# Four experts instead of three loaded in the route stage of a mixture-of-experts kernel, with its tables moved

## The reference

```python
scores = sigmoid(xt @ router)                       # 384 tokens x 64 experts
idx = top 8 of scores + bias, within the 4 best of 8 groups
w = scores[idx] / sum(scores[idx]) * 2.5
routed = sum over the 8 of w * (silu(x @ wg[e]) * (x @ wu[e])) @ wd[e]
x = layernorm(ALPHA * x + gate * (routed + shared expert))
```

## Time and profile before

| | us |
|---|---|
| median of 3 runs | 2140.08 |
| lowest and highest | 2138.03, 2142.44 |
| profiled execution, its own time | 2145.58 |
| its span from first to last instruction | 2143.9 |

### The profile page before, as it was taken

One profiled execution on the slowest core, in us unless ns is written; L12 is line 12 of the kernel. 1 busy time (PEld: TensorE's weight loads), 2 busy tenths in 40 slices (PEclk: granted clock), 3 DMA queues, 4 the chain that ended last, 5 costly groups with the idle time before them and its releaser, 6 DMA issues. The chain is left out here.

```text
span 2143.9 us, 19511 instructions
## 1 busy us (share of the span) xinstructions
PE 1703.3 (79%) x6984; PEld 872.7 (41%) x6984; DVE 696.3 (32%) x1257; ACT 338.9 (16%) x765; POOL 379.5 (18%) x276
## 2 busy tenths in 40 slices
PE   3649788784899997888884578966999978898855
PEld 0117647644444433333331366634444433333321
DVE  0014244767422211111114736485313111111117
ACT  0003162000111111111111215300111111111110
POOL 0000000125111111222215300071111111111115
PEclk8769896585999998999997688976999989999988
DMA  9973001033799999999985401307799999999946
GB/s 370 432 311 115 32 11 45 0 123 155 294 369 405 413 413 407 408 402 398 405 325 208 151 11 40 112 31 292 303 404 408 400 411 404 403 385 390 388 181 236
DMA packets 113716, 589.23 MB, mean 275 GB/s; under 512 B 23152, under 2 KB 25200, under 8 KB 61520
## 3 DMA queue, kind: packets, MB, share of 16 engines
q1 hardware_dynamic: 83088, 512.39, 59.1%
q0 software_dynamic: 30528, 75.55, 9.4%
HBM read 575.09 MB, written 48.41 MB: 291 GB/s over the span
## 5 line engine op out<-in xcount | busy, mean ns | idle before, releaser
L1984 PE MATMUL bank<-weights,scratch 128*64 128x512 f32 x448 | 222.7, 655 | 82.4 <-DMA scratch<-in_moe_w_up 47.5
L2091 DVE TENSOR_TENSOR scratch<-scratch,bank 128x256 f32<-128x256 f32 x88 | 54.0, 614 | 674.5 <-ACT scratch L2059 648.6
L1985 PE MATMUL bank<-scratch 128*64 128x512 f32 x480 | 234.1, 645 | 0.0
L1984 PEld LDWEIGHTS bank<-weights,scratch 128*64 128x64 f32 x448 | 65.1, 151 | 229.0 <-issue 229.0
L1984 PE MATMUL bank<-scratch 128*64 128x512 f32 x288 | 131.9, 612 | 17.8 <-DMA scratch<-in_moe_w_up 17.8
L2059 ACT ACTIVATE scratch<-bank 128x256 f32<-128x256 f32 x88 | 33.7, 383 | 707.8 <-PE bank L1985 427.0
L1990 PE MATMUL bank<-weights,scratch 128*128 128x512 f32 x320 | 141.9, 596 | 2.8 <-ACT scratch L2054 1.7
L1763 POOL DMA_INDIRECT y_rows<-hP,y_idx x42 | 43.5, 1036 | 483.6 <-DVE hP L2096 433.8
L1985 PE MATMUL bank<-weights,scratch 128*64 128x512 f32 x256 | 121.1, 629 | 0.0
L1990 PE MATMUL bank<-scratch 128*128 128x512 f32 x256 | 112.9, 594 | 0.0
L1758 POOL DMA_INDIRECT hP<-h_rows,tok_idx x82 | 85.2, 1040 | 149.0 <-PE bank L1719 85.2
(11 more groups left out here) (320 smaller groups left out, 2846.0 us busy)
## 6 DMA issues: line engine op xcount, KB each, us to landing
weights<-in_moe_w_gate SPq DMA_DIRECT2D x64, 1024.0 KB, 14.5
weights<-in_moe_w_up SPq DMA_DIRECT2D x64, 1024.0 KB, 16.3
weights<-in_moe_w_down SPq DMA_DIRECT2D x64, 1024.0 KB, 21.1
scratch<-in_moe_w_gate SPq DMA_DIRECT2D x64, 1024.0 KB, 12.6
scratch<-in_moe_w_up SPq DMA_DIRECT2D x64, 1024.0 KB, 21.9
scratch<-in_moe_w_down SPq DMA_DIRECT2D x64, 1024.0 KB, 18.8
wmod_more<-in_w_mod SPq DMA_DIRECT2D x9, 3072.0 KB, 32.0
weights<-in_w_mod SPq DMA_DIRECT2D x7, 3072.0 KB
```

Of the source, the lines that this page charges most:

```text
L1984: nc.tensor.matmul(out[0:HALF, :], x[:, 0:HALF], w0[:, kk], start=(kk == 0), stop=(kk == KT - 1))
L1985: m = nc.tensor.matmul(out[HALF:P, :], x[:, HALF:P], w1[:, kk], start=(kk == 0), stop=(kk == KT - 1))
L2091: nc.vector.tensor_tensor(B.h[b % 2].rearrange("p (j q) -> p q j", j=2), B.ex[b % 2].rearrange("p (q j) -> p q j", j=2), k.ps[2 + b % 2][: ...
```

## The change

`FIXED` goes from 3 to 4, with a semaphore of its own for the fourth. Experts 0 to 3 get ranks 0 to 3, the loop in the route stage issues the loads of all four, and the loop in the expert stage begins with place 4. The planner, unchanged itself, puts four experts first and spreads 14 sole experts in place of 15 between the pairs. Since slot 3 is now loaded while the router works, the route tables are moved out of it, to the columns behind the router bias, from 576 on; they must end at column 2816, where slot 2 begins. Their 2092 columns end at 2668.

```diff
-FIXED = 3
-FIXED_SEM = (1, 2, 0)
+FIXED = 4
+FIXED_SEM = (1, 2, 0, 5)
 SOLO = 18
 PAIRS = (NE - SOLO) // 2
...
-        self.s_ahead = [ctx.enter_context(nc.semaphore(f"ahead{i}_loaded")) for i in range(5)]
-        self.ahead = [0] * 5
+        self.s_ahead = [ctx.enter_context(nc.semaphore(f"ahead{i}_loaded")) for i in range(6)]
+        self.ahead = [0] * 6
...
     L = LateTables(k)
-    o = 8960
+    o = MOE_BIAS + NE
...
     Pm = cut(NE)
-    assert o <= 15104, o
+    assert o <= 2816, o
```

## The result

The changed kernel takes 2149.14 us in the median of 7 runs (2147.29 to 2155.74), the kernel before 2141.34 us in the median of 7 (2138.03 to 2145.18). The ratio is 1.0035, with a 95% interval of 1.0018 to 1.0052: slower by 7.5 us (an interval of 3.9 to 11.1 us), where 6 us more were forecast.

A forecast was written before the change was run, and what follows sets the result against it. TensorE was taken to pace the expert stages' opening, DMA the rest. Per layer 1.3 to 5.0 us later, taken as 3.0, gave +6 us for two layers: median 2140.1 to 2146, range 2132 to 2156 (forecast's own 2142.7 to 2150).

The forecast's parts named there:

- No idle DMA time in the route stage: Route stage, 522 to 556 us: DMA engines busy without a gap at 414 GB/s, nothing for a fourth expert to fill.
- The cost of the tables and of SyncE's issues: Route stage: moved tables cost nothing; three more issues take SyncE some 1.5 us, covered by 18 us, so nothing.
- One load earlier: Route stage: of the fourth expert's loads only its down load is truly earlier, 2.5 us more work before the gap.
- The opening, 1.3 us behind: Expert stage's beginning, to 612 us: 25 loads served against 25.5 before, so 0.5 load or 1.3 us behind.
- The shared block, up to 5.0 us behind: Shared block 9, ending about 670 us: 43 loads asked for against 45, a lag of up to 2 loads, 5.0 us.
- my 3.0: Each layer's expert stage: 3.0 us later, taken as about the middle between 1.3 and 5.0 us.
- The order behind block 16 changes nothing: Expert stage from block 17 on: only which of a single and a pair comes first differs; nothing added to the sum.
- The amplified rival: Expert stages: eight places with two pairs in a row, before seven; one more 3.6 us wait per layer; 2153; chance 0.08.
- The lag goes into TensorE's waits: DMA-paced part, after 780 us: TensorE's waits for loads grow by 1 to 5 us per layer, no operation added.
- a sign against me: Expert stages: the prediction would be wrong if TensorE stalls before 780 us or its waits for loads fall.
- The gain: Expert stages: 1 to 3 loads of 2.5 us per layer leave the DMA-paced part; -5 to -15 us; chance 0.18.
- Absorption: DMA-paced part: a DMA lag of 1 to 5 us disappears in the slot-release loops; 2140 us; chance 0.22.

The follow-up runs named there:

- b_order: The kernel before with only the changed order of blocks (four sole experts first), three experts loaded in the route stage, tables unmoved: ratio 1.0033, +7.1 us.
- j_shared9: The changed kernel with the second and third shared tile one block later, behind a pair: ratio 1.0017, +3.6 us against the kernel before.
- c_swap: The changed kernel with the order of the kernel before restored from block 6 on: ratio 1.0019, +4.1 us against the kernel before.
- h_early: The kernel before, three experts loaded in the route stage, with the change's order in blocks 0 to 16 only: ratio 1.0026, +5.6 us.
- i_late: The kernel before, three experts loaded in the route stage, with the change's order in blocks 17 to 43 only: ratio 1.0015, +3.2 us.
- d_change: The changed kernel measured again, on another occasion beside other runs on the same chip, against the kernel before: ratio 1.0041, +8.8 us.
- a_tables: The kernel before with only the route tables moved as in the change, three experts loaded in the route stage: ratio 0.9999, no difference.
- x_full: The kernel before with two more 1 MiB copies per layer, HBM to HBM, issued behind place 40: ratio 1.0040, +8.6 us.
- e_pairs3: The kernel before, three fixed experts, with pairs drawn forward in the order of blocks: ratio 1.0005, +1.1 us.
- g_shared: The kernel before with the second and third shared tiles moved later, to blocks 13 and 17: ratio 0.9996, no difference.

## Why the prediction was right, point by point

**No idle DMA time in the route stage.** Right: the share while the router works is 1.00 before and 1.01 after.

**The cost of the tables and of SyncE's issues.** Nothing, as said. But the three issues took 4.88 + 2.53 + 2.53 = 9.9 us, not 1.5: with that many loads outstanding SyncE is held at the issue itself. It was still covered: the last ends at 532.95 us, and the next issue comes with the stage's beginning, 542 us in this execution.

**One load earlier.** It was counted as 2.5 us more work before the gap, already taken off the opening's lag. b_order, which lacks it, does not differ from the change by more than the noise. One step of this sum is off: with all fifteen loads served at 558.5 us and 2.5 us for each, the twelve queued ones last to 551 us, not 553.5. Nothing rests on it.

**The opening, 1.3 us behind.** Right in sign and size: 0.7 MB (1.7 us) behind in layer 0. The bytes moved in these five stretches are 13.6 MB where I had said 14.0, before 14.6; part of the difference is the 0.2 MB moved early at the higher rate.

**The shared block, up to 5.0 us behind.** Right: 4.7 us behind at its end, and the dip deepened as foretold. With j_shared9, which gives back only this, and c_swap, which restores the late order too, about half of the loss is gone. The whole stage is longer by 4.6, 4.3 and 4.6 us in layer 0 (three profiles with this order) and by 1.7, 4.2 and 3.3 us in layer 1, in the mean 3.8. But this term covers only what is made before block 17, and h_early measures that: 5.6 us, 2.8 per layer (1.6 to 4.0 by its interval), against my 3.0. The 3.0 was a middle between two bounds, so that it fits this well is in part luck.

**The order behind block 16 changes nothing.** Wrong by what the runs show: i_late has +0.15%, 3.2 us (1.1 to 5.4). This term was set at zero. With the 5.6 us of h_early it makes 8.8 us, where the whole change measured 7.5 (3.9 to 11.1); so the sum without it came near the result with some luck. The amplified rival had named the place (an eighth spot of two pairs in a row) and a size of 3.6 us per layer; the size in the runs is 1.6 us per layer. But i_late's order has no more such places than before (seven each), so its mechanism isn't shown.

**The lag goes into TensorE's waits.** Half right. In layer 0 the waits for loads grow by 2.5 us, in layer 1 (49.5 to 49.2 us) not at all, where 1 to 5 us more were foretold for each and a fall was named as a sign against me. Of the 6.3 us, 3.1 are *busy* time of TensorE: 1065.9 us before and 1069.1 after for the same 2135 products per layer. Work behind a wait starts slower. TensorE of the changed kernel around a wait of 5.5 us, in order of time; then two stretches around the same place (columns as in the earlier trace rows):

```profile
886.55 0.59 PE L2016 MATMUL bank<-weights,scratch 128*64 128x512 f32 x1
...
892.66 1.08 PE L1984 MATMUL bank<-weights,scratch 128*64 128x512 f32 x1 [5.51 <-DMA weights<-in_moe_w_up]
```

```profile
888.00:892.60 4.60, 0.00 (x0) 0.00 (x0) 0.00 (x0) 0.00 (x0) 3.75 (x3) 0.63 1.02 415
892.60:895.00 2.40, 2.33 (x6) 0.86 (x8) 0.00 (x0) 0.00 (x0) 0.64 (x1) 0.50 1.02 423
```

The engine has stood idle, the granted clock falls to 0.50 (1.2 of 2.4 GHz), and the first products of the next pair take 1.08 us in place of 0.59. That a wait for DMA makes the clock fall and the next work start slow is also what the Trainium skill says ("TensorE: Matmul & The Clock Gate", section "HAM oscillation — how this bites in real kernels"); this trace agrees, with the 0.50. How the loss is shared between idle and slow time differs from profile to profile (d_change has 530.9 us busy in layer 0 against 530.6 before, and the same 4.6 us of loss), so I had only the sum right.

**A misread row.** I took the wait at 822.00 us for the first one. There is an earlier one, 2.91 us at 782.66. Nothing in the sum rested on it; but the changed kernel then stalls before 780 us, at 766.90 for 1.03 us, which I had named as a sign against me. The sign was badly chosen: a_tables, with the order of before and no loss, stalls at 709.95 us for 0.50 us.

**The rivals.** The gain (0.18) did not come: there was nothing to preload into. Absorption (0.22) came only in part for losses: the lag shrinks from 5.4 to 3.4 us between 130 and 300 us of layer 0, but x_full shows no such relief for its four copies, and the end is later. It did come for leads: e_pairs3 asks for 48 loads by the shared block and not 45, g_shared for 49 by the end of block 9, and neither gains. The argument by loads asked for holds in one direction only, which I had not seen.

## What to carry to other kernels

Before a load is moved ahead, ask whether the transfer engines are idle where it is put, and not only whether the engine that waits is. With a fixed number of buffers, what counts is when each buffer is given back: an item that keeps one buffer for as long as another item keeps two delays all loads behind it, and an item that uses none (here a shared tile) does harm where the next load waits for a buffer that only the item behind it gives back. In this stage, paced by compute early and by transfers later, two copies put in late cost about their full time, and a lead gained early was lost again.

## What the runs showed of the hardware that was not expected

SyncE's issue of a load took 0.33 to 0.65 us for the first twelve loads issued in a row (516.79 to 522.43 us of the changed kernel), and 4.88, 2.53 and 2.53 us for the three behind them. The last two are about what the DMA engines need for one load. A copy of 1 MiB from HBM to HBM cost the saturated stage about as much as a load into on-chip memory: 8.6 us for four by the runs (5.4 to 11.8), 10.2 us by the one profile, so 2.1 to 2.6 us each, where I had allowed for up to twice 2.5.
